# Layer 0's w_q_b and w_kv_b products in three reduced-precision passes instead of one FP32 product

## The reference

```python
for l in range(2):                       # first block
    mod = silu(c) @ w_ada[l] + b_ada[l]  # shift, scale, gate: 3 x 2048
    h = layernorm(x) * (1 + scale) + shift
    u_f, z_f, cq, ckv, k_r, z_a = split(h @ w_in[l])   # 1024,1024,512,256,64,1024
    y_f = fourier_mix(u_f, w_fmix[l]) * silu(z_f)
    q  = rmsnorm(cq, q_norm[l])  @ w_q_b[l]            # 512 x 1536
    kv = rmsnorm(ckv, kv_norm[l]) @ w_kv_b[l]          # 256 x 2048
    # rope on part of q and k, softmax attention of 8 heads, * silu(z_a)
    x = layernorm(ALPHA * x + gate * (concat(y_f, y_a) @ w_out[l]))
```

## Time and profile before

| | us |
|---|---|
| median of three runs | 1605.61 |
| lowest and highest run | 1603.15, 1609.63 |
| the profiled execution | 1604.04 |
| its span, first to last instruction | 1602.2 |
| TensorE matmul busy | 1496.4 (93%) |
| VectorE busy | 1085.6 (68%) |
| ScalarE busy | 707.0 (44%) |
| memory read | 341 MB, 214 GB/s over the span |

### The profile page before, as it was taken

The page is one execution under the profiler, slowest core; times in us unless marked ns, Lnnn a source line. Parts: engine busy times, 40 slices in busy tenths (PEclk is TensorE's granted clock), DMA queues, the critical chain, the costliest instruction groups (busy, mean ns, idle before and its releaser), DMA issues.

```text
span 1602.2 us, 25674 instructions
## 1 busy us (share of the span) xinstructions
PE 1496.4 (93%) x10175; PEld 1332.5 (83%) x10175; DVE 1085.6 (68%) x1890; ACT 707.0 (44%) x1199; POOL 29.6 (2%) x54
## 2 busy tenths in 40 slices
PE   4899999999949999999959999999998999999999
PEld 2677789998849889998849998889987998888987
DVE  3437588989977667676675673885655658887553
ACT  2234235335335445444325444454444546655442
POOL 3000000000000000000000000010000000000000
PEclk8999999999979999999989999999999999999999
DMA  9997878998837565775645554446665553434673
GB/s 366 400 405 250 288 273 302 355 361 332 330 96 241 204 200 179 241 254 195 194 124 185 184 166 145 134 154 220 190 191 159 157 161 112 124 115 122 188 218 105
DMA packets 101416, 345.03 MB, mean 215 GB/s; under 512 B 11213, under 2 KB 21681, under 8 KB 100529
## 3 DMA queue, kind: packets, MB, share of 16 engines
q1 hardware_dynamic: 96880, 327.40, 61.0%
q0 software_dynamic: 4416, 16.00, 2.9%
HBM read 341.16 MB, written 2.20 MB: 214 GB/s over the span
## 4 chain that ended last, share of the span: by engine, by line
PE 74%; DVE 14%; DMA 4%; issue 4%; ACT 3%; SPq 1%; DVEq 0%; ACTq 0%
PE PM L1380 61%; PE PB L1380 9%; DVE wlo L2067 2%; DMA stg<-in_w_in 2%; ACT whi L1744 1%; DVE X L1969 1%; DMA AR<-in_w_in 1%; DVE SM L2302 1%; DVE AC L1969 1%; PE PB L1596 1%; DVE AR L1969 1%; PE PB L1568 1%; ACT AR L1744 1%; DMA stg<-in_w_out 1%; PE PB L1671 1%
## 5 line engine op out<-in xcount | busy, mean ns | idle before, releaser
L2067 DVE TENSOR_TENSOR wlo<-stg,whi 128x1024 fp32r<-128x1024 f32 (+2 forms) x417 | 494.9, 1198 | 315.3 <-ACT whi L1744 313.5
L1744 ACT ACTIVATE whi<-stg 128x1024 fp32r<-128x1024 f32 (+2 forms) x417 | 429.0, 1038 | 417.2 <-PE PM L1380 341.3
L1380 PE MATMUL PM<-Hh,whi 128*128 128x256 f32 x1824 | 528.0, 292 | 8.1 <-DVE Hl L2128 4.9
L1380 PE MATMUL PM<-Hh,wlo 128*128 128x256 f32 x1768 | 497.1, 284 | 0.0
L1380 PE MATMUL PM<-Hl,whi 128*128 128x256 f32 x1824 | 496.8, 284 | 0.0
L1380 PEld LDWEIGHTS PM<-Hh,whi 128*128 128x128 f32 x1824 | 352.5, 193 | 26.3 <-issue 20.7
L1380 PEld LDWEIGHTS PM<-Hl,whi 128*128 128x128 f32 x1824 | 341.9, 192 | 0.5
L1380 PEld LDWEIGHTS PM<-Hh,wlo 128*128 128x128 f32 x1768 | 340.7, 193 | 0.0
L1380 PE MATMUL PM<-whi,Hh 128*128 128x512 f32 (+1 forms) x576 | 223.4, 389 | 0.2 <-DVE Hl L2192 0.2
L1380 PE MATMUL PM<-wlo,Hh 128*128 128x512 f32 (+1 forms) x576 | 220.1, 383 | 0.0
L1380 PE MATMUL PM<-whi,Hl 128*128 128x512 f32 (+1 forms) x576 | 218.4, 384 | 0.0
(11 more groups left out here) (270 smaller groups left out, 1476.5 us busy)
## 6 DMA issues: line engine op xcount, KB each, us to landing
stg<-in_w_ada SPq DMA_DIRECT2D x163, 512.0 KB, 6.2
stg<-in_w_in SPq DMA_DIRECT2D x105, 512.0 KB, 4.8
stg<-in_even_w_in SPq DMA_DIRECT2D x80, 512.0 KB, 3.6
stg<-in_odd_w_in SPq DMA_DIRECT2D x72, 512.0 KB, 3.6
stg<-in_w_out SPq DMA_DIRECT2D x64, 512.0 KB, 4.0
stg<-in_even_w_out SPq DMA_DIRECT2D x32, 512.0 KB, 4.3
stg<-in_odd_w_out SPq DMA_DIRECT2D x32, 512.0 KB, 3.6
AR<-in_w_ada SPq DMA_DIRECT2D x29, 512.0 KB, 10.3
```

Source lines behind the costliest of these rows:

```text
L1380: return e.matmul(out, l, r, start=start, stop=stop, skip_group_check=True)
L1744: return e.activation(out, x, f, **k)
L2067: e.tensor_tensor(wlo[s["slot"]][:, :, 0:n], stg[s["slot"]][:, :, 0:n], whi[s["hi"]][:, :, 0:n].bitcast(F32), ALU.subtract).then_inc(SEM[" ...
```

## The change

In layer 0 the tiles of w_q_b and w_kv_b get a high and a low part, the six normed latent blocks too, and the products are made in three passes, by the code that layer 1 uses. The FP32 branch is gone. The latents stay in `RAW`, their high parts are written by ScalarE to `ARL` and their low parts by VectorE to `ZL`; a wait for the last transposes of layer 0's input is added because ZL lies on Z.

```diff
-            self.jobs.append(dict(mode="split" if split else "raw", src=src(q), n=sum(x[1] for x in src(q)), mm=body, pre=pre if q == 0 else None,
+            self.jobs.append(dict(mode="split", src=src(q), n=sum(x[1] for x in src(q)), mm=body, pre=pre if q == 0 else None,
...
-            a, hh = self.tick("lat", 6), self.tick("lat_hi", 6) if l else None
+            a, hh = self.tick("lat", 6), self.tick("lat_hi", 6)
...
-            Tk["lat"] = self.tick("lat_lo", 2) if l else a
+            Tk["lat"] = self.tick("lat_lo", 2)
...
             if q == 7:
                 self.zw = self.h[KT - 1]
+                self.z_free = ("tr_mm", self.count["tr_mm"])
...
-                elif kind == "direct" and s["split"] is None:
-                    q.wait_all(s["free"])
-                    q.wait_ge(s["ld"])
-                    q.wait_ge(s["lat"])
...
-                elif kind == "lat" and s["l"]:
+                elif kind == "lat":
                     for k in range(6):
                         q.wait_ge((s["lat"][0], s["lat"][1] - 5 + k))
                         act(ARL[:, LAT + k * S:LAT + (k + 1) * S], ar(RAW + k * S, S)).then_inc(SEM["lat_hi"], 1)
...
-                        stt(ar((RAW if s["l"] else LAT) + k * S, S), ar(RAW + k * S, S), VEC[:, g:g + 1], B[:, o:o + S], ALU.mult, ALU.mult).then_inc(
+                        stt(ar(RAW + k * S, S), ar(RAW + k * S, S), VEC[:, g:g + 1], B[:, o:o + S], ALU.mult, ALU.mult).then_inc(
                             SEM["lat"], 1)
-                    if s["l"]:
-                        q.wait_ge(s["lat"])
-                        q.wait_ge(s["z_free"])
-                    for k, n in ((0, 4), (4, 2)) if s["l"] else ():
+                    q.wait_ge(s["lat"])
+                    q.wait_ge(s["z_free"])
+                    for k, n in ((0, 4), (4, 2)):
```

More of the change, by code:

```diff
@@ L248, in group, with direct @@
                                   post=done if q == 7 else None, final=final and q == 7))
-    def direct(self, split, nk, src, units, base, post, Tk, pre=None):
+    def direct(self, nk, src, units, base, post, Tk, pre=None):
         g = {}
@@ L258, in body @@
                 tok = self.tick("mm")
[L259 to L262, removed]
+                self.step("direct", q=q, nk=nk, pair=g["pair"], free=free, split=job["split"], lat=Tk["lat"],
+                          hi=job["hi"], slot=job["slot"], units=units, base=base)
+                self.his.put(job["hi"], tok)
                 self.stgs.put(job["slot"], tok)
@@ L635, in mla @@
         for g in range(4):
-            self.direct(l == 1, 4, lambda q, g=g: q_src(q, g), UQ, 0, q_post(g), Tk, pre=need_lat)
+            self.direct(4, lambda q, g=g: q_src(q, g), UQ, 0, q_post(g), Tk, pre=need_lat)
         def kv_post(g):
@@ L650, in mla @@
         for g in range(4):
-            self.direct(l == 1, 2, lambda q, g=g: [(0, 512, f"w_kv_b{l}", 2 * q, g * 512)], UKV, 4, kv_post(g), Tk)
+            self.direct(2, lambda q, g=g: [(0, 512, f"w_kv_b{l}", 2 * q, g * 512)], UKV, 4, kv_post(g), Tk)
         def heads(h):
@@ L1449, in tensor @@
                                 ins = mm(out, xl[:, kk, tk], wh, False, k == KT - 1)
-                    ins.then_inc(SEM["mm"], 1)
-                elif kind == "direct" and s["split"] is None:
-                    q.wait_all(s["free"])
-                    q.wait_ge(s["ld"])
-                    q.wait_ge(s["lat"])
[L1455 to L1471, removed]
                     ins.then_inc(SEM["mm"], 1)
```

## The result

| | before | changed |
|---|---|---|
| median of six runs each | 1607.65 us | 1614.58 us |
| lowest and highest | 1603.15, 1609.63 | 1612.03, 1618.76 |
| the profiled execution | 1604.04 us | 1612.52 us |
| TensorE, VectorE, ScalarE busy | 1496.4, 1085.6, 707.0 us | 1499.5, 1098.8, 719.0 us |

The changed kernel is slower by 6.9 us, ratio 1.0045 with a 95% interval of 1.003 to 1.0059, so by 0.3 to 0.6%. Three further runs of the kernel before had moved its median up from 1605.61. Both profiled executions are quicker than their medians, by 3.6 us before and 2.1 us in the change.

A forecast was written before the change was run, and what follows sets the result against it. TensorE bounds layer 0 up to 267.10 us, then weight loads: +2.1 (u_out held) +1.4 (clock) -5.8 (products) +7.6 (waits for copies and k) gives 1609.3 profiled, median 1610.9; own range 1608.5 to 1613, overall 1603.5 to 1616.

The forecast's parts named there:

- the hand-over: At 267.10 us in layer 0, where TensorE hands over to VectorE's maximum of a score pair; forecast to move by +5.3.
- the third rival: Slow clock still there or back when the scores start: +8.3 to +9.3 at 267.10, time 1614 to 1615; chance 0.2.
- a microsecond won or lost at 267.10 arrives whole: Any shift where TensorE passes to VectorE's score maximum reaches the end of layer 0 whole, and nothing later takes it back.
- The products, -5.8 us: 80 products of layer 0's q and kv tiles: 0.36 us each instead of 0.432, 5.8 us less on TensorE.
- Step 1: ScalarE's queue: high parts up to q2, waiting for its load, hold u_out; Fourier steps 2.1 us later, stop 3.3 us.
- Step 2: TensorE behind the 3.3 us stop: the clock falls, costing 1.4 us, between 0 and 1.5; q0 starts 3.5 us late.
- Step 3: VectorE from 202.89 us to the third q copy: splits make the copy +5.1, TensorE's rope waiting for it +4.9.
- the second rival: TensorE's gain comes through: copies and splits fit VectorE's pauses, the products' 5.8 us arrive at 267.10, 1599.8; chance 0.1.
- Step 4: Up to the scores: fourth q copy +7.2, its rope at about 227.3, scores +6.9 behind kv3's high part and k copy.
- Step 5: From scores to 267.10: kv1 and kv2 win back 1.1 us, kv3 waits for kv1's copy, TensorE left at +5.3.
- ScalarE did hold u_out: Answers the rival that q2 lands 2 us sooner and u_out isn't held: +1.8 at 267.10, time 1607.4; chance 0.2.
- 11.6 us more for VectorE: Low parts of the twelve tiles on VectorE: 8 of 0.87 and 4 of 1.15 us, 11.6 us in all.

The follow-up runs named there:

- Experiment 1: Changed kernel with the high part of tile q2 moved behind u_out in ScalarE's queue: +1.4 us against the kernel before, ratio 1.0007.
- experiment 10: Changed kernel with six extra FP32 products on TensorE, meant for the wait for u_out but placed behind the first u group: +6.8 us against before.
- experiment 4: Changed kernel without the twelve tiles' low parts on VectorE, the passes reading the high part again: +6.4 us against the kernel before.
- experiment 9: Changed kernel without the twelve low parts and with q2's high part behind u_out in ScalarE's queue: +0.3 us against the kernel before.
- experiment 11: Changed kernel, q2's high part behind u_out, copies ahead of splits, layer 0's q rope and v copies on ScalarE: +0.2 us against before.
- experiment 8: Changed kernel with q2's high part behind u_out and the twelve low parts made by GpSimd instead of VectorE: +7.2 us against before.

## Why the prediction was right, and where a size was off

The forecast was +5.3 us on the profiled execution and so 1610.9 on the median of the time, +5.3 on that too. Measured are +6.9 (4.8 to 9.5 by the interval) for the time and +5.9 for the hand-over. The absolute median came out 3.7 above the forecast: 2.0 of it because the kernel before stood at 1607.65 and not at 1605.61, 1.6 because the difference was too small. So it lies within the range of 1603.5 to 1616 but above this case's own, 1608.5 to 1613, and in absolute terms where the third rival put it.

*What bounds it, "a microsecond won or lost at 267.10 arrives whole".* Right, by the table. The profile seems to say otherwise: from the second maximum to the transposes it is 202.7 us before (470.63 - 267.90) and 205.5 after. But in the other twelve kernels it is 204.1 to 206.6, on either side of the changed one. So the last stop of layer 0 has a shift of 8.1 us (342.74 to 349.11) and the transposes one of 8.7, not 5.9. I take the profiled execution of before to have been lucky behind the hand-over, since its 1604.04 lies well under the median of 1607.65; no second profile of that kernel shows it. I had put it 1.6 us below the median; it was 3.6.

*The products, -5.8 us.* A little too large. The tiles, from start to start, in the changed kernel:

```profile
190.19 0.47 PE L1380 MATMUL PM<-ARL,whi 128*128 128x256 f32 x1
...
192.52 0.61 PE L1380 MATMUL PB<-AR,CF 128*128 128x129 f32 x4
```

q0 takes 2.33 us here, the other q tiles 2.24 to 2.34, where they took 2.59: 0.25 to 0.35 for a tile and not 0.43. Only q6, which follows q5 with nothing between them, takes 2.16. Behind other work the first pass of a tile stands 0.20 to 0.31 us before the second, not 0.12; two passes out of the middle of a tile don't show this. kv1 to kv3 took 10.46 us (225.01 to 235.47) and take 8.90 (230.68 to 239.58): 0.52 for a tile, not 0.58. 8 x 0.3 + 4 x 0.52 is 4.5 us. But much of what the first pass costs is won in the row ahead of it, where the next tile starts sooner: the rope ahead of q3 took 0.50 us from its start to the tile's (202.40 to 202.90) and takes 0.32 (204.19 to 204.51). Six such rows save 0.08 to 0.18 each, 0.8 together. So TensorE was freed of **5.3 us**.

By the four passes of the Trainium skill, FP8 and Floating Point Precision, section TensorE Precision Notes, it would have been 8.6 as an estimate, which the tiles' rows do not bear out. They don't speak against the four passes themselves: 0.432 us a product is four times 0.108. What makes the estimate too large is that a pass of the split takes 0.12.

*Step 1, u_out +2.1, stop 3.3.* Right: u_out's shift is 2.1, the stop 3.21. Experiment 1 shows that the hold is by the instruction's place alone.

*Step 2, the clock, 1.4 between 0 and 1.5.* **This is the term that was mis-sized: 2.8 us.** I took one fall of 3.3 us at the end of the layer for the size of all. Here the slow stretch lasted 5.7 us, through nearly all of the 16 records. Experiment 1 gives both shares of the hold back, 4.9 us in all. q0 was 4.7 late, not 3.5. That the clock's share by itself arrives at the end was not shown, since experiment 10 missed its place.

*Step 3.* Right in kind. VectorE's run starts with a shift of 3.5 (2.2 expected; the clock makes the difference), the third copy has 6.4 (5.1), and the rope waits for just that copy, 3.33 us. The 0.23 us of pause that the second rival puts ahead of the third copy stand behind it; ahead of it VectorE had none.

*Step 4.* The fourth copy's shift is 8.2 (7.2 forecast), its rope's and the scores' 7.4 (6.2, which from the forecast copy should read 6.4, and 6.9). That a clock term 1.4 too small moved the scores by only 0.5 is luck in part: the load of kv3 was issued 1.2 later than forecast, but took 5.7 us to land (220.35 to 226.03), not 6.3. The step named two gates, VectorE's copy and ScalarE's k copy, as if the later one decided. Experiments 4, 9 and 11 show that they stand within 2 us of each other, and that taking away the first gains next to nothing.

*Step 5, +5.3.* 5.9: kv1 to kv3 won 1.6 us back and kv3 did not wait. The maximum of 252.45 had 3.71 us to spare and has 2.65, so VectorE was no bound there, as the step said.

*The rivals.* ScalarE did hold u_out. TensorE's gain didn't come through. The third, a second slow stretch behind the rope's stop, did happen (221 to 224 us, clock 0.52). It ended before the scores, and the wait of 0.36 us behind it shows that VectorE's copy was later anyway. So it cost nothing, by the very condition that the rival gave.

Two terms of the working look large and matter little here. Taking the "11.6 us more for VectorE" away again gives back about 1 us by experiments 1 and 9, since the k copy stands just behind. The waits of TensorE for copies, 4.5 us in the changed kernel, take what its products save and about 1 us more (experiment 1). The rest, 5.5 of the 6.9 us, is one ScalarE instruction that waits for a load.

## What to carry to other kernels

Before adding an instruction to an in-order queue, look at what it waits for and at what stands behind it, not at how long it takes. A 0.84 us high part that waits for a load cost 4.9 us at the hand-over here, and leaving out 11.6 us of work on the busier engine gave back 1. Where an experiment that removes the suspected cost gives nothing back, look for the next gate in the row: the waits ahead of the same consumer (TensorE's rope, its scores, kv3) show it in the same profile.

## What the runs showed of the hardware

- **Stops and the clock.** Over all kernels the 16 Fourier records behind the second u group took 3.72 us behind a stop of 1.17 to 1.60 us, 5.23 behind 2.74, 5.41 behind 3.69, and 6.55 to 6.61 behind 3.21 to 3.81. The scores took 3.06 us behind 0.2 to 0.5 us and 4.59 to 4.74 behind 2.54 to 3.36. What a fall costs varied from 1.5 to 2.9 us, so one fall is no measure for the next. Nor does a fall need a stop of that length: ahead of the layer's first Fourier steps TensorE stops for 0.65 us and then runs a rope and 24 records of one column (from 147.60 us in the kernel before), and the clock fell in eight profiled executions (5.39 us for the 16 records) and stayed up in five (3.70).
- **GpSimd and VectorE.** A GpSimd low part takes 1.8 to 2.4 us in the rows that hold a single one (0.95 to 1.22 on VectorE), and beside it a VectorE instruction with both operands outside PSUM was stretched: 1.69 us instead of 0.41. The Trainium skill, SBUF — State Buffer, section Who interferes with whom, has it that a VectorE instruction with two SBUF inputs contends with a GpSimd instruction that reads SBUF, and that one with at most one such input, outside the two-port modes, does not. The rows of experiment 8 agree with both halves.
- **The first pass of a tile** behind other work costs TensorE 0.20 to 0.31 us from start to start, the following ones 0.12; directly behind another split tile it costs 0.12 too (q6). The row ahead of it is up to 0.19 us shorter than ahead of an FP32 tile (Fourier records to q0: 3.37 us in experiment 1, 3.56 before).
